# Gated linear attention on one core: new engine orders, and every second turned probability tile copied by ScalarE

## Chip, cores and metric

The kernel runs on one core of one Trainium2 chip. The metric is the device time of one launch in microseconds (us), lower is better. Engines are called PE (TensorE), ACT (ScalarE), DVE (VectorE), POOL (GpSimd) and SP (SyncE) below, as the profile calls them.

## The reference, cut to what matters

The program is two layers of a hybrid decoder over 1024 tokens of width 1024. The change lies in the token mixer of the first layer, chunked gated linear attention (GLA) with 4 heads (key width 96, value width 192), which runs in parallel with a 4-head cross-attention into 256 memory tokens:

```python
b = jnp.cumsum(log_a, axis=2)                     # per chunk of 64 tokens
att = einsum('bnihk,bnjhk->bnhij', q * exp(b - b_ref), k * exp(b_ref - b))
o_intra = einsum('bnhij,bnjhv->bnihv', where(tril, att, 0), v)
def step(state, xs):                              # over the chunks
    o = einsum('bchk,bhkv->bchv', qc, state)
    state = dc[..., None] * state + einsum('bchk,bchv->bhkv', kc, vc)
o = rms_norm(o_intra + o_inter, o_norm) * silu(og)
# memory cross-attention, 4 heads of 64, beside it:
p = softmax(einsum('bshd,bmhd->bhsm', q, k) * 64 ** -0.5)
o = einsum('bhsm,bmhd->bshd', p, v)
```

## The kernel before, in words

`gla_phase` (a function of about 430 lines) is one stage of the program, some 180 us of its 2520. Every engine has its own hand-written list of work; they meet only at semaphores. The stage takes the heads h = 0 to 3 in turn.

**PE.** For each head: `gate` (gate projection of the next head, L2508), `token_products` (L2517 within a pair of chunks, L2522 across it), the rest of `project` (L2499, query and key projections of the next heads, in 8 slices d; only for heads 1 and 2, since head 3 is gathered from columns computed with the others), `state_changes` (eight turns of the keys, L2532, then seven products, L2539), `project` again, and `outputs` (fifteen matmuls, L2551 and L2554).

**DVE.** For each head: `cross_pair` (L2417 to L2420), `sums_of` (the log gate L2371, a running sum L2372, two subtractions L2377 and L2378), `low` (the low part of a weight piece, L2366), `states` (L2427, L2429), four `product` calls (L2391, L2393, L2406), `outputs` (L2438, the scaled result).

**ACT.** `gate_in` (L2276, L2277), copies of the scores `att` out of PSUM (L2323), `gate_out` (Exp L2282, Ln L2285), `copy` and `high` (L2266, L2257), copies of the turned keys (L2333), `factor` (Exp, L2294), and the squares of the outputs (L2350). POOL masks `att` (L2237) and computes `rstd` in two halves of each head (L2244, L2246). Exp and Ln each need another table, so ACT loads one where it passes from one to the other.

**Cross-attention** (`CrossUnits`) is cut into 16 units (a unit is 128 tokens and 2 heads) and into 19 steps. In step s PE computes the scores of unit s (L1996), turns the probabilities of unit s-2 with four transposes into one PSUM bank, `t_bank` (L2004), and multiplies unit s-3 with the values (L2013). DVE takes the maximum of unit s (L2021), copies the turned probabilities of unit s-2 out of PSUM (L2029), takes a reciprocal (L2030) and scales unit s-3 (L2036). ACT computes the Exp of unit s (L2048). Since there is one `t_bank`, a turn waits for the copy of the turn before it. The steps are dealt out to places between the GLA work by the table `CROSS`; before, no step stands earlier than after the outputs of head 1:

```python
CROSS = {(1, "out"): range(0, 3), (2, "att"): range(3, 5), (2, "state"): range(5, 8), (2, "out"): range(8, 11),
         (3, "att"): range(11, 13), (3, "state"): range(13, 16), (3, "out"): range(16, CrossUnits.STEPS)}
```

**The ring.** Everything but the projections and the scores of the cross-attention goes through four PSUM banks, taken in turn: entry i waits for whoever frees entry i-4 (`ring_wait`). The two output banks of the first half of a head's outputs and the two of the second half are such entries, freed by DVE's `outputs`.

After the stage comes the output projection (`out_phase`); its first PE work, turns of input rows (L1317), starts when all engines have left the stage.

Of the kernel before, what the change touches and what calls it, by code (L numbers as in the profile page):

```python
# [30 lines left out]
DC = D // P  # L31
# [1938 lines left out]
class CrossUnits:  # L1970
# [8 lines left out]
    def __init__(self, nc, ctx, ph, psum, ident, q_of, keys, vals, out_of, room, sums, banks, out_bank):  # L1979
        def sem(name):  # L1980
            return phase_semaphore(nc, ctx, f"{ph}_{name}")

        self.nc, self.psum, self.ident, self.q_of, self.keys, self.vals, self.out_of = nc, psum, ident, q_of, keys, vals, out_of
        self.probs, self.probs_t, self.banks, self.out_bank = room[0:3], room[3:5], banks, out_bank
        self.neg_top, self.total = sums[:, 0:2 * self.PAIRS], sums[:, 2 * self.PAIRS:4 * self.PAIRS]
        self.scored, self.topped, self.expd = sem("scored"), sem("topped"), sem("expd")
        self.turned, self.turn_out, self.mixed = sem("turned"), sem("turn_out"), sem("mixed")
        self.inverted, self.out_done = sem("inverted"), sem("out_done")

    def pe(self, pe, s, ring_wait):  # L1990
        nc, (s_banks, t_bank) = self.nc, self.banks
        if s < self.PAIRS:
            t, i = divmod(s, 2)
            if s >= 2:
                pe.wait_ge(self.expd, s - 1)
            nc.tensor.matmul(self.psum[:, s_banks[s % 2], :], self.q_of(t, i), self.keys[:, 2 * i:2 * i + 2, :].rearrange("p h n -> p (h n)"),  # L1996
                             start=True, stop=True).then_inc(self.scored, 1)
        u = s - self.T_LAG
        if 0 <= u < self.PAIRS:
            pe.wait_ge(self.expd, u + 1)  # L2000
            if u >= 1:
                pe.wait_ge(self.turn_out, u)
            for c in range(4):
                turn = nc.tensor.transpose(self.psum[:, t_bank, c * P:(c + 1) * P], self.probs[u % 3][:, c, :], self.ident[:, :])  # L2004
            turn.then_inc(self.turned, 1)
        u = s - self.O_LAG
        if 0 <= u < self.PAIRS:
            pe.wait_ge(self.turn_out, u + 1)
            ring_wait(u)
            for e in range(2):  # L2010
                cols = slice((2 * (u % 2) + e) * XA_DIM, (2 * (u % 2) + e + 1) * XA_DIM)
                for c in range(2):
                    mm = nc.tensor.matmul(self.out_bank(u)[:, e * XA_DIM:(e + 1) * XA_DIM], self.probs_t[u % 2][:, 2 * e + c, :],  # L2013
                                          self.vals[:, c, cols], start=c == 0, stop=c == 1)
            mm.then_inc(self.mixed, 1)

    def dve(self, dve, s):
# [6 lines left out]
        if 0 <= u < self.PAIRS:  # L2024
            two = slice(2 * u, 2 * u + 2)
            dve.wait_ge(self.turned, u + 1)
            if u >= 2:
                dve.wait_ge(self.mixed, u - 1)
            nc.vector.tensor_copy(self.probs_t[u % 2], self.psum[:, t_bank, :].rearrange("p (c n) -> p c n", c=4)).then_inc(self.turn_out, 1)  # L2029
            nc.vector.reciprocal(self.total[:, two], self.total[:, two]).then_inc(self.inverted, 1)  # L2030
# [8 lines left out]
    def act(self, act, s):  # L2039
        if s >= self.PAIRS:  # L2040
            return
        act.wait_ge(self.topped, s + 1)
# [10 lines left out]
def gla_phase(nc, ph, psum, ident, neg_half, hT_hi, hT_lo, w_in, w_gate2, b_gate, rank_rows, V, Y, room, first_parts, last_rows, cross_room, pieces,  # L2053
# [10 lines left out]
    with ExitStack() as ctx:  # L2064
# [3 lines left out]
        def sem(name):  # L2068
# [53 lines left out]

        CROSS = {(1, "out"): range(0, 3), (2, "att"): range(3, 5), (2, "state"): range(5, 8), (2, "out"): range(8, 11),
                 (3, "att"): range(11, 13), (3, "state"): range(13, 16), (3, "out"): range(16, CrossUnits.STEPS)}

# [30 lines left out]
        for h in range(GLA_HEADS):  # L2156
            if h + 1 < GLA_HEADS:
                enter("z", "act", 2, h + 1)
            enter("att", "act", 2, h)
            enter("cross", "dve", 1, h)  # L2160
            enter_cross(h, "att")
            enter("keys", "act", 2, h)
            enter("delta", "state", 4, h)
            enter_cross(h, "state")
            enter("out", "dve", 4, h)
            enter_cross(h, "out")
# [16 lines left out]

        def at(h, kind, i=0):
            return entry_of[h, kind] + i

# [64 lines left out]
        def _(act):  # L2251
# [62 lines left out]
            for h in range(GLA_HEADS):  # L2314
# [21 lines left out]
                if more:  # L2336
                    factor(h + 1, 0)
                    factor(h + 1, 1)
                cross_steps(cross.act, act, h, "state")
                if fresh:  # L2340
                    copy(h + 1, 1)
                if h + 2 < LAST:
                    high(2 * h + 4)
                if h:
# [10 lines left out]
        def _(dve):  # L2355
# [11 lines left out]

            def sums_of(h):

                dve.wait_ge(softened, h + 1)  # L2370
                chain(nc.vector.scalar_tensor_tensor(soft, z, 0.0, soft, ALU.min, ALU.subtract))  # L2371
                chain(nc.vector.tensor_tensor_scan(cum, keep, soft, 0.0, ALU.mult, ALU.add))  # L2372
                c = cum.rearrange("p (c i) -> p c i", i=CHUNK)
# [58 lines left out]

            def outputs(h):
                for p in range(PAIRS):
                    if p % (PAIRS // 2) == 0:
                        dve.wait_ge(rstd_ready, 2 * h + 1 + p // (PAIRS // 2))
                    y = Y[:, p, h * DV:(h + 1) * DV]
# [4 lines left out]

            dve.wait_ge(kept, 2)
            sums_of(0)
            low(2)
# [3 lines left out]
            product(0, 3)  # L2449
            for h in range(GLA_HEADS):  # L2450
                more = h + 1 < GLA_HEADS
                fresh = h + 1 < LAST
                cross_pair(h)
                cross_steps(cross.dve, dve, h, "att")
                if more:
                    sums_of(h + 1)
                if fresh:
                    low(2 * h + 3)
                states(h)
                cross_steps(cross.dve, dve, h, "state")  # L2460
                if more:
                    product(h + 1, 0)
                if h + 2 < LAST:
                    low(2 * h + 4)
                if more:
                    product(h + 1, 1)
                outputs(h)
                if more:
                    product(h + 1, 2)
                    product(h + 1, 3)  # L2470
                if h == 1:
                    for part in range(2):
                        dve.wait_ge(parked[part], 16 * LAST)
                cross_steps(cross.dve, dve, h, "out")

        @block.tensor
        def _(pe):
# [47 lines left out]

            def state_changes(h):
                pe.wait_ge(factored, h + 1)
                for i in range(2):
                    ring_wait(at(h, "keys", i))
                    for c in range(4):  # L2530
                        p = 4 * i + c
                        mm = nc.tensor.transpose(bank(at(h, "keys", i))[:, c * DK:(c + 1) * DK], k_out[:, p * P:(p + 1) * P], ident[0:DK, 0:DK])  # L2532
                    mm.then_inc(mixed, 1)
                for p in range(PAIRS - 1):
                    i = at(h, "delta", p // 2)
# [7 lines left out]

            def outputs(h):
                pe.wait_ge(masked, h + 1)
                for p in range(PAIRS):
                    i = at(h, "out", p // 2)
# [21 lines left out]
            for h in range(GLA_HEADS):  # L2569
                if h + 1 < GLA_HEADS:  # L2570
                    gate(h + 1)
                token_products(h)
                if h + 1 < LAST:
                    project(2 * h + 2, range(EARLY, DC))
                cross_at(h, "att")
                state_changes(h)
                cross_at(h, "state")
                if h + 1 < LAST:
                    project(2 * h + 3)
                outputs(h)  # L2580
# [723 lines left out]
```

## Time and profile before

| | us |
|---|---|
| median of 3 runs | 2525.84 |
| lowest, highest of the runs | 2524.62, 2526.70 |
| profiled execution, its time | 2521.81 |
| profiled execution, its span | 2520.00 |
| head loop of the stage starts (PE) | 248.15 |
| first cross-attention scores (PE) | 316.43 |
| last DVE instruction of the stage ends | 405.47 |

The span is the time from the first to the last instruction on the core; the execution's own time is 1.81 us longer. The rows further down are from the trace of that one execution. "Idle before" is the time in which an engine stood still ahead of an instruction, with the instruction that released it. The granted clock is 1.00 where PE had its full clock (2.4 GHz) and 0.50 where it had the lower level (1.2 GHz).

### The profile page before, as it was taken

How to read it: one execution, taken by the hardware profiler on the slowest of the kernel's cores; microseconds unless marked ns; L12 is line 12 of the kernel's file. 1: busy time of each engine (PE TensorE's matmuls, PEld its weight loads, DVE VectorE, ACT ScalarE, POOL GpSimd, SP SyncE). 2: the span in 40 equal slices, each digit the busy share in tenths (PEclk: the TensorE clock that was granted, in tenths of full speed). 3: DMA queues.
4: the chain of work that ended last, by engine and by line, in shares of the span. 5: the costliest groups of instructions: out<-in, count | busy, mean ns of one | idle time of the engine just before them, and what ended most of it. 6: DMA issues, size and time to landing. Idle time of an engine off the chain costs nothing. (4 is left out here: it accounts for less than half of the span.)

```text
span 2520.0 us, 32372 instructions
## 1 busy us (share of the span) xinstructions
PE 2432.4 (97%) x11700; PEld 2055.1 (82%) x11700; DVE 1729.7 (69%) x2908; ACT 1033.7 (41%) x2126; POOL 225.7 (9%) x271
## 2 busy tenths in 40 slices
PE   7999979999999999998999999999899999999998
PEld 7998757888888887777889889887788888888777
DVE  4532564379899888885553562463669999898896
ACT  6433443344444443335434432333334444443443
POOL 1010021000000000041212021122100000000000
PEclk9999988999999999999999999999999999999999
DMA  4330121322222248743102011212532222226764
GB/s 149 89 89 22 39 79 43 100 69 84 76 92 84 75 142 272 262 142 130 51 17 81 35 34 42 60 34 73 168 115 75 85 84 83 77 91 221 280 200 146
DMA packets 207541, 257.72 MB, mean 102 GB/s; under 512 B 38376, under 2 KB 141784, under 8 KB 207384
## 3 DMA queue, kind: packets, MB, share of 16 engines
q1 hardware_dynamic: 203224, 255.65, 31.0%
q8 instruction: 94, 1.54, 0.3%
q10 hardware_dynamic: 4160, 0.02, 0.1%
q14 instruction: 63, 0.52, 0.1%
HBM read 206.54 MB, written 49.09 MB: 101 GB/s over the span
## 5 line engine op out<-in xcount | busy, mean ns | idle before, releaser
L52 PE MATMUL psum<-f_T_lo 128*128 128x512 f32 x616 | 244.6, 397 | 13.0 <-DVE f_T_lo L676 11.9
L53 PE MATMUL psum<-f_T_lo 128*128 128x512 f32 x616 | 241.3, 392 | 0.0
L54 PE MATMUL psum<-f_T_lo 128*128 128x512 f32 x616 | 241.2, 392 | 0.0
L52 PE MATMUL psum<-w_hi,hT_hi 128*128 128x512 f32 x576 | 229.3, 398 | 4.2 <-DVE w_lo L1445 2.5
L54 PE MATMUL psum<-w_hi,hT_lo 128*128 128x512 f32 x576 | 226.3, 393 | 0.0
L53 PE MATMUL psum<-w_lo,hT_hi 128*128 128x512 f32 x576 | 226.1, 393 | 0.0
L52 PEld LDWEIGHTS psum<-f_T_lo 128*128 128x128 f32 x616 | 116.4, 189 | 48.1 <-DVE f_T_lo L676 21.1
L52 PEld LDWEIGHTS psum<-w_hi,hT_hi 128*128 128x128 f32 x576 | 124.8, 217 | 22.4 <-issue 3.9
L54 PEld LDWEIGHTS psum<-w_hi,hT_lo 128*128 128x128 f32 x576 | 125.0, 217 | 17.9
L53 PEld LDWEIGHTS psum<-w_lo,hT_hi 128*128 128x128 f32 x576 | 125.1, 217 | 16.6
L52 PE MATMUL psum<-hT_hi,f_up_hi 128*128 128x512 f32 x352 | 137.4, 390 | 0.4 <-DVE f_up_lo L615 0.4
L54 PE MATMUL psum<-hT_hi,f_up_lo 128*128 128x512 f32 x352 | 137.0, 389 | 0.0
L53 PE MATMUL psum<-hT_lo,f_up_hi 128*128 128x512 f32 x352 | 137.0, 389 | 0.0
L54 PEld LDWEIGHTS psum<-f_T_lo 128*128 128x128 f32 x616 | 116.4, 189 | 25.0
L53 PEld LDWEIGHTS psum<-f_T_lo 128*128 128x128 f32 x616 | 116.4, 189 | 23.1
L52 PE MATMUL psum<-T_hi,f_s_hi 128*128 128x512 f32 x320 | 124.5, 389 | 0.0
L53 PE MATMUL psum<-f_T_lo,f_s_hi 128*128 128x512 f32 x320 | 124.5, 389 | 0.0
L54 PE MATMUL psum<-T_hi,f_s_lo 128*128 128x512 f32 x320 | 124.5, 389 | 0.0
L52 PE MATMUL psum<-T_hi,f_up_hi 128*128 128x512 f32 x320 | 124.5, 389 | 0.0
L53 PE MATMUL psum<-f_T_lo,f_up_hi 128*128 128x512 f32 x320 | 124.5, 389 | 0.0
L54 PE MATMUL psum<-T_hi,f_up_lo 128*128 128x512 f32 x320 | 124.5, 389 | 0.0
L455 ACT ACTIVATE f_T_lo<-f_up_pieces 128x1024 fp32r<-128x1024 f32 (+1 forms) x72 | 67.0, 957 | 119.1 <-PE psum L54 101.9
(416 smaller groups left out, 6087.7 us busy)
## 6 DMA issues: line engine op xcount, KB each, us to landing
raw<-in_ffn_w_up_dram SPq DMA_DIRECT2D x88, 512.0 KB, 4.7
activations<-f_act SPq DMA_DIRECT2D x44, 512.0 KB, 2.6
f_up_pieces<-activations SPq DMA_DIRECT2D x38, 512.0 KB, 4.4
w_raw<-in_b_w_in_dram SPq DMA_DIRECT2D x18, 1024.0 KB, 5.9
f_up_pieces<-in_ffn_w_down_dram SPq DMA_DIRECT2D x20, 512.0 KB, 4.8
x_between<-XY SPq DMA_DIRECT2D x16, 512.0 KB, 5.2
XY<-x_between SPq DMA_DIRECT2D x16, 512.0 KB, 6.5
f_up_pieces<-activations SPq DMA_DIRECT2D x28, 256.0 KB, 3.9
```

What stands on the lines that cost most here:

```text
L52: nc.tensor.matmul(out, lhs_hi, rhs_hi, start=start, stop=False)
L53: nc.tensor.matmul(out, lhs_hi, rhs_lo, start=False, stop=False)
L54: return nc.tensor.matmul(out, lhs_lo, rhs_hi, start=False, stop=stop)
L455: nc.scalar.activation(hi, raw, ACT.Copy).then_inc(b_high, 1)
```

## The change

- `CrossUnits`: the copy of the turned probabilities stays on DVE for even units and goes to ACT (an activation with Copy) for odd units. The semaphore `turn_out` becomes two, one for even and one for odd units. On ACT the copy of unit s-2 stands behind the Exp of unit s.
- The steps move: 0 and 1 go between the two halves of the outputs of head 1 (new place "half"), step 2 stays behind them; steps 5 and 13 go to a new place "keys", between the turns of the keys and the state products; step 16 goes between the halves of the outputs of head 3.
- PE: `state_changes` is split; the keys are turned (`turn_keys`) before the last slice of the first projection of a head, and `outputs` comes in halves.
- ACT: the key copies come before `copy` and `high`; for head 3, `factor` moves between the squares of the two halves of head 2's outputs; the cross steps of "att" come before the key copies.
- DVE: `sums_of` is split (`logs_of`), the outputs come in halves with products 2 and 3 between them for heads 0 and 1, and for heads 2 and 3 the order is written out.

```diff
+    def wait_turn_out(self, eng, u):
+        eng.wait_ge(self.turn_out[u % 2], u // 2 + 1)
...
             if u >= 1:
-                pe.wait_ge(self.turn_out, u)
+                self.wait_turn_out(pe, u - 1)
...
-            dve.wait_ge(self.turned, u + 1)
-            if u >= 2:
-                dve.wait_ge(self.mixed, u - 1)
-            nc.vector.tensor_copy(self.probs_t[u % 2], ...).then_inc(self.turn_out, 1)
+            if u % 2 == 0:
+                dve.wait_ge(self.turned, u + 1)
+                if u >= 2:
+                    dve.wait_ge(self.mixed, u - 1)
+                nc.vector.tensor_copy(self.probs_t[0], self.turned_tile()).then_inc(self.turn_out[0], 1)
+            else:
+                dve.wait_ge(self.expd, u + 1)
...
     def act(self, act, s):
+        u = s - self.T_LAG
+        if s < self.PAIRS:
+            self.act_exp(act, s)
+        if 0 <= u < self.PAIRS and u % 2:
+            act.wait_ge(self.turned, u + 1)
+            if u >= 2:
+                act.wait_ge(self.mixed, u - 1)
+            self.nc.scalar.activation(self.probs_t[1], self.turned_tile(), ACT.Copy).then_inc(self.turn_out[1], 1)
...
+        CROSS = {(1, "half"): range(0, 2), (1, "out"): range(2, 3), (2, "att"): range(3, 5), (2, "keys"): range(5, 6), (2, "state"): range(6, 8),
+                 (2, "out"): range(8, 11), (3, "att"): range(11, 13), (3, "keys"): range(13, 14), (3, "state"): range(14, 16),
+                 (3, "half"): range(16, 17), (3, "out"): range(17, CrossUnits.STEPS)}
...
-                if fresh:
-                    copy(h + 1, 0)
-                    high(2 * h + 3)
+                cross_steps(cross.act, act, h, "att")
...
-                cross_steps(cross.act, act, h, "att")
-                if more:
+                if fresh:
+                    high(2 * h + 3)
+                    copy(h + 1, 0)
+                cross_steps(cross.act, act, h, "keys")
+                if fresh:
                     factor(h + 1, 0)
                     factor(h + 1, 1)
...
+                    if p == PAIRS // 2:
+                        if more and not fresh:
+                            factor(h + 1, 0)
+                            factor(h + 1, 1)
+                        cross_steps(cross.act, act, h, "half")
...
+            for h in range(LAST - 1):
                 cross_pair(h)
+                logs_of(h + 1)
+                sums_of(h + 1)
+                low(2 * h + 3)
                 states(h)
+                product(h + 1, 0)
                 if h + 2 < LAST:
                     low(2 * h + 4)
+                product(h + 1, 1)
+                cross_steps(cross.dve, dve, h, "half")
+                outputs(h, 0)
+                product(h + 1, 2)
+                product(h + 1, 3)
+                outputs(h, 1)
...
+            cross_steps(cross.dve, dve, LAST - 2, "out")
+            first, second, third = CROSS[LAST - 1, "out"]
+            cross_pair(LAST - 1)
+            cross_steps(cross.dve, dve, LAST - 1, "att")
+            cross_steps(cross.dve, dve, LAST - 1, "keys")
+            logs_of(LAST)
+            states(LAST - 1)
+            cross.dve(dve, CROSS[LAST - 1, "state"][0])
+            sums_of(LAST)
+            cross.dve(dve, CROSS[LAST - 1, "state"][1])
+            outputs(LAST - 1, 0)
+            product(LAST, 0)
+            cross.dve(dve, first)
+            product(LAST, 1)
+            outputs(LAST - 1, 1)
+            cross.dve(dve, second)
+            product(LAST, 2)
+            product(LAST, 3)
+            cross.dve(dve, third)
+            cross_pair(LAST)
...
...
-                if h + 1 < LAST:
-                    project(2 * h + 2, range(EARLY, DC))
+                if fresh:
+                    project(2 * h + 2, range(EARLY, DC - 1))
                 cross_at(h, "att")
+                turn_keys(h)
+                if fresh:
+                    project(2 * h + 2, range(DC - 1, DC))
+                cross_at(h, "keys")
                 state_changes(h)
                 cross_at(h, "state")
...
-                outputs(h)
+                outputs(h, 0)
                 if h == 1:
                     pe.wait_ge(copied, 2 * LAST)
                     pe.wait_ge(kv_loaded, 16 * len(kv_loads))
+                cross_at(h, "half")
+                outputs(h, 1)
                 cross_at(h, "out")
```

## Rows read from the trace of the kernel before

**Rows 1.** The page, busy time of each engine over the whole span.
```profile
PE 2432.4 (97%) x11700; PEld 2055.1 (82%) x11700; DVE 1729.7 (69%) x2908; ACT 1033.7 (41%) x2126; POOL 225.7 (9%) x271
```

**Rows 2.** Windows: us, busy us (instructions) of each engine, granted clock.
```profile
316.40:330.70 14.30, 8.39 (x16) 2.93 (x14) 7.54 (x16) 4.95 (x18) 8.17 (x6) 0.68 0.84 321
330.70:355.10 24.40, 21.57 (x125) 16.99 (x125) 16.81 (x32) 14.56 (x32) 1.10 (x1) 0.84 0.00 1
```

**Rows 3.** Timeline of PE: start, duration, work, idle before in brackets.
```profile
261.38 2.49 PE L2539 MATMUL psum<-gla_v,gla_k_rows 128*96 128x192 f32 x14 [1.87 <-ACT gla_k_rows L2333]
...
316.43 1.88 PE L1996 MATMUL psum<-kv_room,xqT 128*128 128x512 f32 x4
324.22 2.08 PE L1996 MATMUL psum<-kv_room,xqT 128*128 128x512 f32 x2 [5.91 <-ACT cross_room L2048]
...
330.73 3.78 PE L2517 MATMUL psum<-gla_q_mid,gla_k_mid 96*128 96x128 f32 x16
...
367.48 1.08 PE L2004 MATMUL psum<-ident,cross_room 128*128 128x128 f32 x4 [4.21 <-DVE cross_room L2029]
...
373.55 2.00 PE L2517 MATMUL psum<-gla_q_mid,gla_k_mid 96*128 96x128 f32 x16
...
400.75 1.08 PE L2004 MATMUL psum<-ident,cross_room 128*128 128x128 f32 x4 [2.79 <-DVE cross_room L2029]
...
405.80 1.94 PE L1317 MATMUL psum<-ident,XY 128*128 128x128 f32 x8 [0.65 <-PEq L2064]
```

**Rows 4.** Timeline of PE, one undisturbed cross-attention step at full clock.
```profile
385.61 0.60 PE L2004 MATMUL psum<-ident,cross_room 128*128 128x128 f32 x4
386.05 1.00 PE L2013 MATMUL psum<-kv_room,cross_room 128*128 128x64 f32 x8
386.89 1.08 PE L1996 MATMUL psum<-kv_room,xqT 128*128 128x512 f32 x2
```

**Rows 5.** Windows of 2 us; the clock is the third last figure.
```profile
338.00:340.00 2.00, 2.00 (x14) 1.75 (x13) 1.80 (x5) 0.46 (x1) 1.10 (x1) 0.83 0.00 0
...
346.00:348.00 2.00, 1.32 (x6) 0.56 (x5) 1.93 (x5) 1.39 (x5) 0.00 (x0) 1.00 0.00 0
...
372.00:374.00 2.00, 2.00 (x16) 2.00 (x16) 1.71 (x4) 1.02 (x4) 0.00 (x0) 0.80 0.00 0
```

**Rows 6.** Timeline of DVE.
```profile
261.00 1.21 DVE L2366 TENSOR_TENSOR mem_lo<-kv_room,mem_lo 128x1024 fp32r<-128x1024 f32 x1
...
322.43 1.28 DVE L2021 TENSOR_REDUCE rank_rows<-psum 128x2 f32<-128x512 f32 x2
...
405.18 0.29 DVE L2036 TENSOR_TENSOR XY<-psum,rank_rows 128x128 f32<-128x128 f32 x1 [1.41 <-PE psum L2013]
```

**Rows 7.** Timeline of POOL.
```profile
317.73 1.01 POOL L2246 TENSOR_TENSOR gla_rstd<-gla_sums,neg_half 128x4 f32<-128x4 f32 x1
```

**Rows 8.** Groups of ACT, 316.4 to 405.8 us: busy, mean ns | idle.
```profile
L2048 ACT ACTIVATE cross_room<-psum,rank_rows 128x256 f32<-128x256 f32 x32 | 14.8, 473 | 25.0 <-DVE rank_rows L2021 25.0
L2323 ACT ACTIVATE gla_att<-psum 128x512 f32<-128x512 f32 x4 | 2.4, 597 | 3.1 <-PE psum L2517 3.1
L2276 ACT ACTIVATE raw<-psum,gla_bias 96x512 f32<-96x512 f32 x2 | 1.4, 683 | 1.5 <-PE psum L2508 1.5
L2285 ACT ACT_TABLE_LOAD x1 | 1.3, 1283 | 0.0
L2285 ACT ACTIVATE gla_soft<-gla_soft 96x1024 f32<-96x1024 f32 x1 | 1.1, 1057 | 0.0
```

**Rows 9.** Groups of DVE, 316.4 to 405.8 us.
```profile
L2429 DVE SCALAR_TENSOR_TENSOR gla_state<-gla_state,gla_decay,psum 96x192 f32<-96x192 f32 x12 | 4.9, 410 | 0.4
L2029 DVE COPY cross_room<-psum 128x512 f32<-128x512 f32 x8 | 5.5, 686 | 0.3 <-PE psum L2004 0.3
L2406 DVE TENSOR_TENSOR gla_k_out<-gla_k_mid,gla_ends 96x1024 f32<-96x1024 f32 x2 | 2.4, 1216 | 0.0
L2372 DVE TENSOR_TENSOR_SCAN raw<-gla_keep,gla_soft 96x1024 f32<-96x1024 f32 x1 | 2.3, 2286 | 0.0
```

More of the change, by code:

```diff
@@ L1986, in __init__, with turned_tile @@
         self.scored, self.topped, self.expd = sem("scored"), sem("topped"), sem("expd")
-        self.turned, self.turn_out, self.mixed = sem("turned"), sem("turn_out"), sem("mixed")
+        self.turned, self.mixed = sem("turned"), sem("mixed")
+        self.turn_out = [sem(f"turn_out_{n}") for n in ("even", "odd")]
         self.inverted, self.out_done = sem("inverted"), sem("out_done")
+    def wait_turn_out(self, eng, u):
+        eng.wait_ge(self.turn_out[u % 2], u // 2 + 1)
+    def turned_tile(self):
+        return self.psum[:, self.banks[1], :].rearrange("p (c n) -> p c n", c=4)
     def pe(self, pe, s, ring_wait):
@@ L2162, in gla_phase @@
             enter("keys", "act", 2, h)
+            enter_cross(h, "keys")
             enter("delta", "state", 4, h)
             enter_cross(h, "state")
-            enter("out", "dve", 4, h)
+            enter("out", "dve", 2, h)
+            enter_cross(h, "half")
+            enter("out_end", "dve", 2, h)
             enter_cross(h, "out")
@@ L2184, in at @@
         def at(h, kind, i=0):
+            if kind == "out" and i >= 2:
+                return entry_of[h, "out_end"] + i - 2
             return entry_of[h, kind] + i
@@ L2343, in _ @@
                     high(2 * h + 4)
+                cross_steps(cross.act, act, h, "state")
                 if h:
@@ L2431, in states, with outputs @@
                     dve.wait_ge(state_ready, (PAIRS - 1) * h + p + 1)
-            def outputs(h):
-                for p in range(PAIRS):
+            def outputs(h, half):
+                for p in range(half * PAIRS // 2, (half + 1) * PAIRS // 2):
                     if p % (PAIRS // 2) == 0:
-                        dve.wait_ge(rstd_ready, 2 * h + 1 + p // (PAIRS // 2))
+                        dve.wait_ge(rstd_ready, 2 * h + 1 + half)
                     y = Y[:, p, h * DV:(h + 1) * DV]
@@ L2443, in _ @@
             dve.wait_ge(kept, 2)
+            logs_of(0)
             sums_of(0)
@@ L2463, in _ @@
                 if h + 2 < LAST:
                     low(2 * h + 4)
-                if more:
-                    product(h + 1, 1)
-                outputs(h)
[L2468 to L2474, printed above, removed]
+                product(h + 1, 1)
+                cross_steps(cross.dve, dve, h, "half")
@@ new lines, in _ @@
+                outputs(h, 0)
+                product(h + 1, 2)
+                product(h + 1, 3)
+                outputs(h, 1)
+            for part in range(2):
+                dve.wait_ge(parked[part], 16 * LAST)
+            cross_steps(cross.dve, dve, LAST - 2, "out")
[4 more added lines that the diff above has]
+            logs_of(LAST)
@@ new lines, in _ @@
+            states(LAST - 1)
[12 more added lines that the diff above has]
+            cross_pair(LAST)
+            cross_steps(cross.dve, dve, LAST, "att")
@@ L2476, in _ @@
+            cross_steps(cross.dve, dve, LAST, "keys")
+            states(LAST)
+            cross_steps(cross.dve, dve, LAST, "state")
+            cross_steps(cross.dve, dve, LAST, "half")
+            outputs(LAST, 0)
+            cross.dve(dve, CROSS[LAST, "out"][0])
+            outputs(LAST, 1)
+            cross.dve(dve, CROSS[LAST, "out"][1])
         @block.tensor
@@ L2542, in state_changes, with outputs @@
                         mm.then_inc(mixed, 1)
-            def outputs(h):
+            def outputs(h, half):
                 pe.wait_ge(masked, h + 1)
-                for p in range(PAIRS):
+                for p in range(half * PAIRS // 2, (half + 1) * PAIRS // 2):
                     i = at(h, "out", p // 2)
```

31 lines of the change are left out of this document (8 added, 23 removed).

## The prediction, made before the changed kernel was run

> **What bounds the kernel now.** I read the page first: PE is busy 97% of the span [rows 1], so a gain has to be PE time won, and since the later stages keep PE full, time won in this stage passes through to the end. Next the windows of the stage. Up to 316.4 us PE is nearly full; from 316.4 to 330.7 it is busy 8.4 of 14.3 us at a mean clock of 0.68, and the next 24.4 us have 0.84 [rows 2]. PE's timeline shows why [rows 3]: a wait of 1.87 us for the key copies at 261.38 (the same again in head 1), one of 5.91 us at 324.22 for ACT's first Exp, of 4.21 us at 367.48 and of 2.79 us at 400.75 for DVE's copy. The first big one is DVE's fault: PE has issued scores 0 and 1 by 318.3, but DVE takes the first maximum at 322.43 [rows 6], after the outputs and two products of head 1. Third, the clock: after the waits of 5.91 and 4.21 us the work runs at half clock (score pairs 2.08 instead of 1.08 us, rows 3 and 4 compared) [rows 3, 4], and the full clock is back only at 338.7 and 372.8 (from the means 0.83 and 0.80 of their windows) [rows 5]. A wait thus costs itself and half of the slow stretch behind it.
>
> **The change, part by part.** I walk the queues from head to head with durations from the rows, 0.05 us a handoff.
>
> *Keys turned early (heads 0 and 1).* The last slice of the projection (six matmuls, 1.36 us) now covers ACT's two key copies, so the 1.87 us [rows 3] go. What is late next is `project` 3, which waits for `low`: that ends at 262.2, because its DVE predecessors are unchanged [rows 6]. The state products now end at 261.55, so PE stands 0.7 us: gain 1.3 us (263.57 to 262.26). Head 1 starts 1.3 earlier, its keys give 1.3 again: 2.6 us. Bounds: 0 if `low` slips by as much, 3.7 if it never waits.
>
> *Steps 0 and 1 between the output halves of head 1.* The first half of the outputs ends on PE at 311.2. The memory keys must have landed by then: before, PE showed no wait for them at 316.43 [rows 3], so a late landing can cost at most the 5.2 us between. Scores 0 and 1 run 311.2 to 313.2, DVE's maxima 312.4 to 313.9, the Exps to 314.9, while PE does the second half (to 315.75). DVE then has outputs, products 2 and 3 (2 x 1.14 us apart) [rows 9], and waits for the second `rstd`: squares end 316.6, POOL takes 1.01 [rows 7] and two short steps, so outputs end at 319.4. PE goes from step 2 (with a turn) through the gate projection to `token_products` of head 2 at 319.0, against 330.73 [rows 3]: 11.7 us gained so far, the 2.6 included, because the wait of 5.91 and its half clock are gone. If the `rstd` wait moved the whole of it back, 5 would remain.
>
> *The odd copy on ACT: a new wait.* One copy of 128x512 costs DVE 0.69 us; ACT's copies of that shape took 0.60 [rows 8, 9]. The copy itself is cheap; its place isn't. Maximum 2 comes at 320.1 (behind the outputs), Exp 2 to 321.05. ACT then has `gate_in` (four of 0.68, 2.3 with overlap), two score copies (1.1), `gate_out` (Exp, a table of 1.28, Ln 1.06: 3.4), a table load of 1.28, Exp 3 (two halves 0.47 and their reads: 0.9) [rows 8], and only then the copy of unit 1, done at 330.65. The turn of unit 2 needs it, since there is one `t_bank`; behind that turn stand, in PE's queue, unit 1's product, the key turns and everything of head 2. PE has nothing from 325.3 on: a new wait of 5.4 us. DVE waits too, for the turn, with unit 2's copy. Before, this copy was DVE's and `gate_out` overlapped with step 3. Bounds: 2 us if ACT's work is spread better than I think, 7 if handoffs are slow.
>
> *What the new wait does to the clock.* 5.4 us lies between the 4.21 and 5.91 that both lost the clock. The slow busy stretch was 5.3 us behind the one and 14.5 behind the other [rows 3, 5]; what follows here (turn, product, scores) is like the shorter case. From 330.7 at half clock for 5.3 us costs 2.7; I take 8 us of it, 4. Ends: 0 (the clock stays) and 7.
>
> *Head 2's rest.* `logs_of` before `states`, `sums_of` (2.29 scan, a short and a long subtraction, 3.6) [rows 9] after step 6. With 2.7 of clock loss: states 339.4 to 342.4 (seven of 0.4 in sequence [rows 9]), maximum 6, copy 4, running sums to 347.5, maximum 7, Exp 7 at 349.05, ACT copy 5, squares of the first half to 350.85, `factor` 2.5 to 353.35, squares to 354.55, second `rstd` at 355.9. PE meanwhile has outputs to 349.9, then waits of 1.7 (unit 5's product for a ring bank that DVE's outputs free), 1.3 (for copy 6), and 2.7 (for copy 7, which is behind Exp 9, behind maximum 9, behind DVE's outputs). `token_products` of head 3 start at 362.3, against 373.55: 11.2 ahead.
>
> *Head 3 and the tail.* Steps 11 to 18 are PE-bound at about 2.2 us (0.43 + 0.84 + 0.93, starts in [rows 4]), but for 1.2 at step 12 waiting for ACT's copy 9. Step 16's place hides what waited 2.79 us and then ran at half clock at 400.75 [rows 3]. DVE ends at 391.1, against 405.47 [rows 6]: 14.4 ahead. The row turns that follow (1.94 us at half clock [rows 3]) may find full clock: 0.9. The added semaphore, the reciprocals and POOL's mask (1.1 us, 15 us of slack) I cost at nothing; POOL's weight splits cover more of the stage but end before they are needed.
>
> *The sum.* 14.4 + 0.9 = 15.3; minus 1.3 for the longer slow stretch, minus 1 for handoffs I count low over some 20 links: **13.0 us**. Against the profiled execution's own 2521.81 that is 2508.8. The median of the runs lies 4.0 above that execution, so the same gain gives 2525.84 - 13.0 = **2512.8**.
>
> *A rule against it.* Gaps of 1.56 us and less in a stretch that was 66% busy left the clock at 1.00 (1.32 of 2 us) [rows 5]; the new order has 1.7, 1.3 and 2.7 close together between 350 and 361. The Trainium skill, TensorE: Matmul & The Clock Gate, section "A second HAM failure mode: psum-queue depth-cycling", says that frequent micro-idles between matmul groups that cycle through PSUM banks make the clock oscillate. By that rule the cross steps from 331 on would run mostly slow; rival 3 prices it, and the row so far speaks against it.
>
> **Rivals.**
> 1. *The clock is lost a second time*, at the 2.7 us wait for copy 7 near 361. For it: 2.79 us at 400.75 was followed by half clock (4 turns 1.08) [rows 3]. Against: the wait at 346 to 348 wasn't. At half clock for 5 to 8 us: 2.5 to 4 more, gain 7 to 11, about 2516.5.
> 2. *No clock loss at the first wait*, or a shorter wait since ACT overlaps more: 13.0 + 4 gives 17, 2508.8. Against: both waits over 4 us lost it.
> 3. *The clock stays low, and the kernel gets slower.* Place: all PE work after 330.7, which by my list is 47 us at full clock with 9 us of waits in it. Slow work swallows the waits. It decides from the point where over 62% of the 47 us run at half clock: 330.7 + 47 x 1.62 + 3 = 410, past 405.5 + 5. With all of it slow, 330.7 + 94 + 3 = 428, 22 us late: 2548. Against it: 342 to 355 had waits every few us and kept 1.00 after 340.
> 4. *The change gives little* (it doesn't do what it says): each of the 8 odd copies waits out its Exp and itself (0.9 + 0.6, 1.5 us), 12 us, with none hidden, and steps 0 and 1 still stall on DVE. Then 1 to 5 us are left, about 2523. Against: in the walk only copies 1, 7 and 9 are seen by PE.
>
> **How the numbers follow.** Likeliest case (gain 11 to 16) 0.50; rival 1 0.26; rival 2 (16 to 19) 0.12; rival 3 0.04; rival 4 0.08, half of it inside 0.2%. 0.2% is 5 us, which is about what a measurement of this kernel can tell from no change. The range from a gain of 7 to one of 19 holds the first three: 2507 to 2519. Faster by over 0.2%: 0.50 + 0.26 + 0.12 + 0.03 = 0.91; within: 0.05; slower: 0.04.
>
> **What the profile after would show.** Right: `token_products` of head 2 near 319, and ahead of it no wait over 1 us; key-copy waits under 1 us; one PE wait of about 5.4 us before a turn (L2004's code) near 325 to 331, released by the Copy on ACT; half clock behind it; full clock from about 339; three waits under 3 us between 350 and 361; head 3's `token_products` near 362; the next stage's turns near 391. Wrong: a wait at the memory keys' semaphore; the turn of unit 2 released before 328; half clock through the 350s; a later stage longer than before, which none of my terms has.

## The result and the profile after

The changed kernel takes 2507.31 us (median of 7 runs, 2504.89 to 2512.37) against 2524.62 (7 runs, 2516.76 to 2526.70). The ratio is 0.9942, 95% interval 0.9931 to 0.9953: 14.6 us faster, between 11.9 and 17.4. In the profiled executions the span went from 2520.0 to 2505.8 us, 14.2 less. The next stage's first PE work starts at 391.74 instead of 405.80 [rows 3], 14.1 earlier, so in these two profiles the gain was won before that point. Below this number is called the *stage mark*.

On the page after, PE is busy 2428.7 us, 97% of the span again, against 2432.4 [rows 1]:

```profile
PE 2428.7 (97%) x11700; PEld 2053.4 (82%) x11700; DVE 1725.7 (69%) x2900; ACT 1036.6 (41%) x2134; POOL 226.0 (9%) x271
```

The work is the same. Eight copies changed sides (DVE 2908 to 2900 instructions, ACT 2126 to 2134). Here is PE's timeline after, with its waits in the stage but for two of 0.20 and 0.33 us. The number in brackets is the idle time ahead. L2573 is the old L2517, L2012 are the turns, L2021 the products with the values, L2555 the projections:

```profile
264.88 0.73 PE L2555 MATMUL psum<-h_hi,mem_lo 128*128 128x512 f32 x2 [0.19 <-DVE mem_lo L2397]
300.44 0.73 PE L2555 MATMUL psum<-h_hi,mem_lo 128*128 128x512 f32 x2 [0.41 <-DVE mem_lo L2397]
322.06 3.15 PE L2573 MATMUL psum<-gla_q_mid,gla_k_mid 96*128 96x128 f32 x16 [0.65 <-DVE XY L2470]
333.75 0.63 PE L2012 MATMUL psum<-ident,cross_room 128*128 128x128 f32 x4 [2.04 <-ACT gla_v L2058]
344.04 0.63 PE L2012 MATMUL psum<-ident,cross_room 128*128 128x128 f32 x4 [0.64 <-DVE cross_room L2038]
353.39 1.08 PE L2021 MATMUL psum<-kv_room,gla_v 128*128 128x64 f32 x8 [1.63 <-DVE XY L2470]
356.37 0.63 PE L2012 MATMUL psum<-ident,cross_room 128*128 128x128 f32 x4 [0.98 <-DVE cross_room L2038]
361.19 0.63 PE L2012 MATMUL psum<-ident,cross_room 128*128 128x128 f32 x4 [2.45 <-ACT gla_v L2058]
369.78 0.63 PE L2012 MATMUL psum<-ident,cross_room 128*128 128x128 f32 x4 [0.96 <-ACT gla_v L2058]
391.74 1.94 PE L1317 MATMUL psum<-ident,XY 128*128 128x128 f32 x8 [1.68 <-PEq L2083]
```

The waits of 1.87 (twice), 5.91, 4.21 and 2.79 us [rows 3] are gone. In their place stand three behind ACT's new copies (2.04, 2.45, 0.96, released by L2058) and two over 0.7 us behind DVE (1.63 and 0.98). Windows of 2 us show where the clock was lost before the tail of the stage (the clock is the third figure from the end):

```profile
250.00:252.00 2.00, 2.00 (x15) 2.00 (x15) 0.00 (x0) 2.00 (x4) 0.00 (x0) 0.76 0.00 0
252.00:254.00 2.00, 2.00 (x18) 1.78 (x17) 0.00 (x0) 1.51 (x3) 0.00 (x0) 0.50 0.00 0
...
322.00:324.00 2.00, 1.94 (x12) 1.97 (x13) 1.83 (x5) 0.80 (x3) 1.10 (x2) 0.68 1.03 418
324.00:326.00 2.00, 1.80 (x12) 1.50 (x11) 0.00 (x0) 2.00 (x6) 2.00 (x1) 0.50 1.02 420
...
332.00:334.00 2.00, 0.25 (x2) 0.28 (x3) 0.89 (x4) 1.99 (x9) 0.67 (x1) 1.00 0.00 0
```

It was lost where PE had no gap (at 251, 2.00 of 2.00 us busy) or a short one (0.65 us ahead of 322.06), and not at the wait before 333.75, where PE was busy 0.25 of 2 us; from 334 to 390 us it stayed at 1.00. That is not how I had it. A second profile of the same kernel (after_again, below) shows what I had forecast: the clock lost behind the wait.

### The profile page after: what moved, and what is told of

It is laid out like the page before. It is cut to its first block and busy times, and to the rows that moved or that the text cites. A ratio compares the mean times of both kernels' runs of the same rounds, so it can differ in the third digit from the quotient of the medians.

```text
span 2505.8 us, 32380 instructions
## 1 busy us (share of the span) xinstructions
PE 2428.7 (97%) x11700; PEld 2053.4 (82%) x11700; DVE 1725.7 (69%) x2900; ACT 1036.6 (41%) x2134; POOL 226.0 (9%) x271
```

## The experiments

Times are given as the ratio to the kernel before, measured beside it on the same chip. The median of before was between 2520.5 and 2524.6 us, so 0.001 is 2.5 us. The stage mark comes from one profile each and contains that execution's luck with the clock. Names that end in "_again" are the same kernel measured a second time.

| kernel | ratio (95% interval) | stage mark | head 2's, head 3's token products |
|---|---|---|---|
| before | 1 | 405.80 | 330.73, 373.55 |
| changed | 0.9942 (0.9931 to 0.9953) | 391.74 | 322.06, 362.50 |
| after_again | 0.9958 (0.9944 to 0.9973) | 395.82 | 319.34, 363.28 |
| keys_early_only | 0.9984 (0.9973 to 0.9995) | 407.74 | 330.98, 375.49 |
| half_only | 0.9984 (0.9973 to 0.9995) | 400.78 | 323.77, 368.54 |
| only_act_copy | 1.0028 (1.0014 to 1.0043) | 408.48 | 330.46, 375.68 |
| all_copies_dve | 0.9922 (0.9904 to 0.9941) | 385.02 | 319.31, 356.73 |
| all_copies_dve_again | 0.9924 (0.9911 to 0.9938) | 388.36 | 319.34, 357.10 |
| copy_first | 0.9913 (0.9899 to 0.9928) | 384.45 | 319.44, 355.92 |
| copy_first_again | 0.9909 (0.9896 to 0.9923) | 383.28 | 319.42, 354.75 |
| gate_late | 0.9919 (0.9905 to 0.9933) | 387.10 | 322.18, 358.56 |
| step3_first | 0.9960 (0.9948 to 0.9972) | 393.56 | 319.21, 358.99 |
| splits_later | 0.9941 (0.9926 to 0.9956) | 396.18 | 319.69, 363.61 |
| waits_filled | 0.9941 (0.9928 to 0.9953) | 388.96 | 319.41, 359.73 |

**One part alone: the keys.** The lists of PE and ACT in short:

```diff
 PE: -  project(2 * h + 2, range(EARLY, DC)); cross_at(h, "att"); state_changes(h)
     +  project(2 * h + 2, range(EARLY, DC - 1)); cross_at(h, "att"); turn_keys(h)
     +  project(2 * h + 2, range(DC - 1, DC)); state_changes(h)
 ACT: -  copy(h + 1, 0); high(2 * h + 3); key copies
      +  key copies; high(2 * h + 3); copy(h + 1, 0)
```

> The kernel before with the keys turned ahead of the last projection slice (PE), and ACT's key copies ahead of its copy of the projection. Theory 1: both waits of 1.87 us go and 0.2 to 0.7 us for the low part comes instead, 1.3 us for each head, 2.6 us faster in all, since PE is full up to 316. Rival (the project call that follows is late by as much): 0. A difference of 2.6 us is 0.1% and near what the runs can tell, so the trace decides: the start of head 1's second projection and the start of the first scores, 316.4 before.

Measured: 0.16% faster, 1.3 to 6.8 us. In its profile the key waits are gone, but the clock fell near 251 us with PE full, so that single trace shows no earlier second projection of head 1 (300.78 us). In after_again, where it didn't fall there, that projection starts at 297.70, against 300.48 in the kernel before (its timeline): 2.8 us. Up to there the changed kernel differs in the place of the keys and in the orders of ACT and DVE around them, so the term of 2.6 stands.

**One part alone: steps 0 and 1.**

```diff
-CROSS = {(1, "out"): range(0, 3), ...
+CROSS = {(1, "half"): range(0, 2), (1, "out"): range(2, 3), ...
 DVE, head 1:
-  outputs(h); product(h + 1, 2); product(h + 1, 3)
+  steps of "half"; outputs(h, first half); product(h + 1, 2); product(h + 1, 3); outputs(h, second half)
```

> The kernel before with cross steps 0 and 1 between the output halves of head 1, on all three engines, DVE's outputs of that head in halves around products 2 and 3. Theory 1: the wait of 5.9 us and most of the half clock behind it go; head 2's token products start 8 to 9 us earlier, near 322; 7 to 10 us faster at the end. Rival (the stall is only moved: DVE's outputs are late, PE waits for ring banks): token products of head 2 after 327 and less than 4 us faster.

Measured: 0.16% faster, 4.0 us (1.3 to 6.8), less than the 7 to 10 expected. The token products of head 2 do start 7.0 us earlier, nearly as theory 1 says, in spite of a stretch at half clock near 263. Of these, 2.0 are given back by the stage mark (5.0 earlier). PE's timeline:

```profile
323.77 2.02 PE L2526 MATMUL psum<-gla_q_mid,gla_k_mid 96*128 96x128 f32 x16 [0.65 <-DVE XY L2440]
327.13 1.15 PE L2531 MATMUL psum<-gla_q_in,gla_k_out 96*64 96x64 f32 x16 [1.33 <-ACT gla_soft L2277]
334.35 1.09 PE L2004 MATMUL psum<-ident,cross_room 128*128 128x128 f32 x4 [2.83 <-DVE gla_v L2029]
...
362.45 1.09 PE L2004 MATMUL psum<-ident,cross_room 128*128 128x128 f32 x4 [4.21 <-DVE cross_room L2029]
```

A head start puts PE ahead of the engines that feed it: two new waits (1.33 for the gate's reads on ACT, 2.83 for DVE's copy 1), and a turn of 1.09 us, half clock, behind the second. The later waits of 4.21 and 2.79 stay as they were. They are gone in the changed kernel and, with every copy on DVE, in all_copies_dve too, so it is the orders of heads 2 and 3 that take them away.

No run has these orders alone. By subtraction they are the largest part: with all copies on DVE the new orders bring 19 to 20 us (ratios 0.9922 and 0.9924, below), and the two parts above brought 4.0 each by themselves, which leaves 11 to 12 us. That is an estimate from these ratios, and it holds only if the parts add up.

**One part alone, and one part undone: the copies on ACT.** only_act_copy has the odd copies on ACT in the old orders (with ACT's cross steps of "att" ahead of the key copies; left where they were, the engines would wait for one another); all_copies_dve is the changed kernel with no copy on ACT:

```diff
+    def on_act(self, u):
+        return False
...
-            if u % 2 == 0:
+            if not self.on_act(u):
```

> The kernel before with odd copies on ACT, and for that ACT's cross steps of the place att moved ahead of its key copies (with the old place the engines would wait for one another). Nothing else moved. Theory 1: the wait of 5.9 us for Exp 0 and the half clock behind it stay; copies 1, 7 and 9 are late behind Exps, copy 0 stays on DVE: between 3 us slower and 2 us faster than before. Rival: 5 us or more faster.

> The changed kernel with every copy of turned probabilities back on DVE; all new orders kept. Theory 1 (the orders bring the gain, the ACT copy costs PE a wait and saves DVE 0.69 us eight times): the wait of 2.04 us for ACT's copy 1 goes, but Exp 3 still ends near 333 behind the gate work, so PE waits there one step later, 1 to 2 us; between 350 and 361 DVE is the late engine and gets copies 5 and 7 (1.3 us) more. Sum within 2 us of the changed kernel, 12 to 16 us under the kernel before. Rival (the ACT copy is what brings the gain): 5 us or more of the 14.6 are lost, 2514 or more where the kernel before has 2524.

Both speak against the copy on ACT. Alone it makes the kernel 0.28% slower (3.5 to 10.8 us; I had between 2 faster and 3 slower). Undone, the changed kernel gains: 0.9922, then 0.9924, against 0.9942 and 0.9958. These were measured on different chips, each beside the kernel before, and the lower interval of the changed kernel touches the other two; but every pairing points the same way, by some 4 to 9 us. My "within 2 us" was wrong. The rival, that this copy brings the gain, has fallen.

PE's wait before the turn of unit 2 doesn't go with ACT's copy. It is now for DVE's copy of unit 1, 2.19 us in the first profile (0.69 in the second, where PE was at half clock just before), and the turn starts earlier, at 329.24 instead of 331.03 in after_again. The wait for copy 7 is 1.51 instead of 2.45:

```profile
329.24 0.63 PE L2015 MATMUL psum<-ident,cross_room 128*128 128x128 f32 x4 [2.19 <-DVE gla_v L2041]
...
355.42 0.63 PE L2015 MATMUL psum<-ident,cross_room 128*128 128x128 f32 x4 [1.51 <-DVE gla_v L2041]
```

> All copies on DVE once more, beside copy_first. If the place of the copy in its queue is what counts and not the engine, the two are within 2 us of each other, and both 5 to 11 us faster than the changed kernel.

**The changed kernel again.**

> The changed kernel once more, for a second profile beside the others of this call. Theory 1 says that the stage starts its last turns (next stage's first PE work) at 391.7 us less whatever the clock does differently: the half clock at 251 to 257 us of the first profile is chance, so 389 to 392. If ACT's copies cost more than they save (all copies on DVE gave 0.9922), the ratio stays above 0.993.

The ratio of 0.9958 is 10.6 us (6.8 to 14.1) against 14.6 in the first measurement, and above 0.993 as expected. The stage mark of 395.82 lies outside the 389 to 392 that I gave: its trace shows that the first profile's mark was on the lucky side. PE's timeline, and then the clock in 2 us windows:

```profile
322.69 1.15 PE L2578 MATMUL psum<-gla_q_in,gla_k_out 96*64 96x64 f32 x16 [1.32 <-ACT gla_soft L2303]
331.03 0.63 PE L2012 MATMUL psum<-ident,cross_room 128*128 128x128 f32 x4 [3.95 <-ACT gla_v L2058]
...
361.63 0.63 PE L2012 MATMUL psum<-ident,cross_room 128*128 128x128 f32 x4 [2.45 <-ACT gla_v L2058]
...
395.82 1.14 PE L1317 MATMUL psum<-ident,XY 128*128 128x128 f32 x8 [1.67 <-PEq L2083]
```
```profile
330.00:332.00 2.00, 0.97 (x9) 1.00 (x9) 0.30 (x1) 1.80 (x7) 0.00 (x0) 0.96 0.00 0
332.00:334.00 2.00, 2.00 (x13) 2.00 (x13) 0.75 (x3) 0.27 (x1) 0.00 (x0) 0.50 0.00 0
...
338.00:340.00 2.00, 2.00 (x13) 1.96 (x13) 1.44 (x3) 0.31 (x1) 0.00 (x0) 0.84 0.00 0
...
362.00:364.00 2.00, 2.00 (x14) 2.00 (x13) 2.00 (x5) 0.81 (x3) 0.00 (x0) 0.64 0.00 0
...
372.00:374.00 2.00, 2.00 (x10) 1.47 (x10) 0.29 (x1) 1.19 (x5) 1.91 (x3) 0.80 0.00 0
```

With the clock up at 319, PE reaches the wait for copy 1 earlier and waits 3.95 us; half clock follows from about 331.8 to 338.6 (worked out from the window means). It comes again after the wait of 2.45, from about 362.6 to 372.8. Both waits stand behind ACT's copy. In this execution each cost itself and half of the seven or ten microseconds at half clock. splits_later, below, whose PE list is the same, has the same two waits and the same two slow stretches.

**Where the copy stands in ACT's queue.** In the changed kernel ACT's list around copy 1 is this (timeline, reads of the accumulator left out):

```profile
327.34 1.08 ACT L2308 ACTIVATE gla_soft<-gla_soft 96x1024 f32<-96x1024 f32 x1
328.44 1.28 ACT L2311 ACT_TABLE_LOAD   x1
329.73 1.06 ACT L2311 ACTIVATE gla_soft<-gla_soft 96x1024 f32<-96x1024 f32 x1
330.81 1.28 ACT L2067 ACT_TABLE_LOAD   x1
332.10 0.47 ACT L2067 ACTIVATE cross_room<-psum,rank_rows 128x256 f32<-128x256 f32 x1
...
333.01 0.59 ACT L2058 ACTIVATE gla_v<-psum 128x512 f32<-128x512 f32 x1
```

The copy loads no table of its own: here it follows an Exp directly, and in gate_late, below, one runs behind Ln (337.33 us) ahead of the next load (337.93). In this list it stands behind two loads of 1.28 us, and behind Exp 3. copy_first swaps the two of a step:

```diff
     def act(self, act, s):
         u = s - self.T_LAG
-        if s < self.PAIRS:
-            self.act_exp(act, s)
         if 0 <= u < self.PAIRS and u % 2:
             ... copy of unit u
+        if s < self.PAIRS:
+            self.act_exp(act, s)
```

> The changed kernel, but ACT takes the odd copy ahead of the Exp of the same step. Theory 1 (PE waits for copies 7 and 9 only because they stand behind Exps 9 and 11, which wait for DVE's maxima): the waits of 2.45 and 0.96 us go, copy 1 comes 1 us sooner, 2.5 to 4.5 us faster than the changed kernel. Rival (the Exps are then late instead, since each turn comes half a microsecond behind its scores): within 1 us of it.

> copy_first once more, for a second profile with the clock in another state. Theory 1: ratio 0.990 to 0.993; where the clock stays up before head 2's token products, PE waits 1 to 2 us for copy 1, and no copy after it makes PE wait over 1 us.

Measured: 0.9913 and 0.9909, some 7 to 12 us faster than the changed kernel (11 us in the one comparison on the same chip, 0.9913 against 0.9958), more than the 2.5 to 4.5 expected. The waits for copies 7 and 9 are gone in both profiles; the one for copy 1 is gone in the first and 1.61 in the second (PE's timeline):

```profile
328.78 0.63 PE L2012 MATMUL psum<-ident,cross_room 128*128 128x128 f32 x4 [1.61 <-ACT gla_v L2056]
339.41 0.63 PE L2012 MATMUL psum<-ident,cross_room 128*128 128x128 f32 x4 [0.64 <-DVE cross_room L2038]
348.28 1.08 PE L2021 MATMUL psum<-kv_room,gla_v 128*128 128x64 f32 x8 [1.15 <-DVE XY L2470]
```

The second profile has the full clock from 310 to 382 us, where after_again had two slow stretches; its mark is 12.5 us earlier. That is probably the difference to my number: I counted the waits, not the slow stretches behind them. The kernel with the copy first has the lowest ratios of the study, with medians of 2499.24 and 2500.15 us. Between it and all copies on DVE (0.9922, 0.9924) the runs don't decide: they are 2.3 and 3.8 us apart, not within the 2 that I expected, and the intervals overlap.

**The gate moved instead.** step3_first takes Exp 3 and copy 1 ahead of `gate_out` (and moves POOL's splits of weights as splits_later does, so it changes two things); gate_late is copy_first with steps 3, 4 and the key copies ahead of `gate_out` of head 3. ACT's lists in short:

```diff
 step3_first, ACT, head 2:  -gate_out(3); step 3; step 4; key copies
                            +step 3; gate_out(3); step 4; key copies
 gate_late, ACT, head 2:    -gate_out(3); step 3; step 4; key copies; step 5
                            +step 3; step 4; key copies; gate_out(3); step 5
```

> The changed kernel, but ACT takes step 3 (Exp 3, copy 1) ahead of gate_out of head 3, and POOL takes one weight split behind the mask of head 2 and three behind that of head 3 in place of two behind head 1's second rstd. Theory 1 (copy 1 is late because of gate_out and its two table loads): PE's wait before the turn of unit 2 (2.04 us) shrinks to under 1 us, and token products of head 3 start 1 to 3 us sooner after those of head 2. Rival (DVE's maximum 3 sets it): the wait stays over 1.5 us.

> Copy ahead of Exp as in copy_first, and for head 2 ACT does steps 3 and 4 and the key copies before gate_out of head 3. Theory 1: PE has no wait over 1 us between head 2's token products and its outputs, which start near 338 (345.3 in the changed kernel); DVE's logs wait for the late gate. 1 to 5 us faster than copy_first. Rival (the late gate delays sums, maximum 7, squares and factor, which set the later waits): token products of head 3 start no sooner than in copy_first, same time.

In step3_first the wait for copy 1 is 0.96 us, as theory 1 says, but the key copies now stand behind the gate and PE waits 1.73 us for them, and loses the clock there and again behind the wait of 2.45 that is left. From head 2's token products to head 3's it takes 39.8 us, against 40.4 and 43.9 in the two profiles of the changed kernel, but the kernel isn't faster (0.9960). gate_late removes the waits for copy 1 and for the keys, and has no gain over copy_first (0.9919). Head 2's outputs start at 344.52, not near 338. Ahead of them PE waits 1.33 for a ring bank that ACT's `gate_in` frees, 0.98 for a state and 1.56 for DVE's copy 4, with half clock behind the last; the two later ones fit logs that come late, which wasn't tested by itself. The outcome is the rival's: from head 2's token products to head 3's it is 36.4 us, and 36.5 and 35.3 in copy_first. That they start at 322.18 against 319.42 comes from a stretch at half clock from about 286.5 to 293 us.

**POOL against DVE.** POOL splits weights of a later stage (L1116, L1118) at the same place in both kernels. In the kernel before, DVE's first multiplication of `cross_pair` for head 2 came at 336.45, seven microseconds behind the last of them. With head 2 earlier, the two meet. The two timelines of the changed kernel, DVE first:

```profile
327.41 2.82 DVE L2449 TENSOR_TENSOR gla_q_in<-gla_q_in,gla_ends 96x512 f32<-96x512 f32 x1 [3.58 <-PE psum L2578]
```
```profile
327.34 2.34 POOL L1118 TENSOR_TENSOR h_lo<-o_w_stage,h_hi 128x1024 fp32r<-128x1024 f32 x1
```

splits_later moves the splits:

```diff
-SPLITS = {(1, "rstd"): range(0, 2), (3, "mask"): range(2, 4)}
+SPLITS = {(2, "mask"): range(0, 1), (3, "mask"): range(1, 4)}
```

> The changed kernel with only POOL's weight splits moved: one behind the mask of head 2, three behind that of head 3. In the changed kernel DVE's first multiplication of cross_pair of head 2 took 2.82 us in place of 0.69 while POOL ran a tensor_tensor of 2.34 us. If the two hold each other up, it is back at 0.69 here. Theory 1 (ACT is later still, so the 2.1 us are hidden): time within 1 us of the changed kernel. Rival (they are on the path): 2 us faster.

The same multiplication takes 0.69 us in this kernel (the row is below). The ratio, 0.9941, is that of the changed kernel within the intervals, and PE's wait for copy 1 is 3.95 us with the splits in the way (after_again) and without (this run): the delay was hidden behind ACT's later copy.

```profile
324.22 0.69 DVE L2449 TENSOR_TENSOR gla_q_in<-gla_q_in,gla_ends 96x512 f32<-96x512 f32 x1 [2.77 <-PE psum L2578]
```

**What a wait costs beyond itself.** waits_filled keeps PE at work in the waits for copies 1 and 7, with four and two more score products whose results nobody reads:

```diff
         pe.wait_ge(self.expd, u + 1)
+        for _ in range({4: 4, 10: 2}.get(s, 0)):
+            nc.tensor.matmul(self.psum[:, 2, :], self.q_of(0, 0), self.keys[:, 0:2, :]..., start=True, stop=True)
         if u >= 1:
             self.wait_turn_out(pe, u - 1)
```

> The changed kernel with spare work in two of PE's waits: four score products (0.93 us each) ahead of the wait for copy 1 and two ahead of the wait for copy 7, into a PSUM bank that nobody uses then and with results nobody reads. Nothing waits less. Theory 1 (a wait costs itself and the half clock behind it): the waits of 3.95 and 2.45 us shrink to under 0.6, the clock stays at 1.00 from 332 to 374 us, and the kernel is 3 to 8 us faster than the changed one though it does more work. Rival (the waits alone cost, and the clock falls by chance): same time, or slower by 1.

```profile
326.99 3.60 PE L2010 MATMUL psum<-kv_room,xqT 128*128 128x512 f32 x8
331.01 0.66 PE L2014 MATMUL psum<-ident,cross_room 128*128 128x128 f32 x4 [0.42 <-ACT gla_v L2060]
...
355.87 1.88 PE L2010 MATMUL psum<-kv_room,xqT 128*128 128x512 f32 x4
358.39 0.66 PE L2014 MATMUL psum<-ident,cross_room 128*128 128x128 f32 x4 [0.64 <-ACT gla_v L2060]
```

The turn of unit 2 starts at 331.01 as in after_again (331.03): the release is the same. But the clock stays at 1.00 from there to 388, head 3's token products start 3.6 us earlier than in after_again and the stage mark is 6.9 us earlier. Between these two traces, then, the two slow stretches are worth about 7 us. One trace of each doesn't show that filling the waits is what kept the clock: in the changed kernel's first profile neither wait lost it (the first was 2.04 us there). Nor do the runs: 0.9941 stands against 0.9942 and 0.9958, no difference that can be told, where I expected 3 to 8 us. Theory 1 isn't shown, and the rival isn't excluded.

A count over all fourteen profiles says more about which waits pay. It takes each wait of PE from the start of the stage to the stage mark (the one that ends at the mark left out), and asks whether the granted clock was at 0.50 two microseconds after PE's return:

| wait of PE | waits | half clock behind them |
|---|---|---|
| 3.95 to 5.91 us | 9 | 9 |
| 2.45 to 2.83 us | 10 | 8 |
| 1.51 to 2.19 us | 20 | 5 |
| 1.00 to 1.33 us | 13 | 0 |

So the price of a wait is paid in some executions and not in others, and in these profiles it was paid more often the longer the wait. The count shows what goes together, not the cause.

## Why the prediction was right, point by point

*The number.* 2512.8 was forecast with a range of 2507 to 2519, 13.0 us faster; measured 2507.31 and 14.6 by the ratio. The absolute time is 5.5 us lower than forecast, only 0.3 us inside the range: the median of the kernel before is itself 1.2 us lower in its 7 runs than in the first 3, and the two medians lie 17.3 us apart where the ratio gives 14.6. The second measurement of the same kernel gave 10.6, so the forecast of 13.0 lies between the two.

*Keys early, 2.6 us.* 2.8 in the profile that kept its clock there (after_again). The new wait for `low` is 0.42 and 0.41 in it; I had 0.7 for the first.

*Steps 0 and 1, token products of head 2 at 319.0.* 319.34 in after_again; 322.06 in the first profile, 2.7 later because of the half clock at 251 to 257 (second `project` of head 0 at 264.88 against 262.13). Alone, in the old orders, this part was worth 4.0 us where the expectation for half_only said 7 to 10. In the prediction's walk it was the first 9 of the 14 us; what the walk doesn't say is that without the later orders PE only runs into the next waits.

*The new wait for copy 1, 5.4 us.* Placed right, sized too long: 3.95 us where PE came to it at full clock. The walk missed that `token_products` waits 1.32 us for a ring bank that ACT's `gate_in` frees, so PE comes later to the wait (the row at 322.69 us above); the copy itself came within 0.4 us of the 330.65 forecast.

*Half clock behind it, 8 us.* 6.8 us in after_again, from 331.8 to 338.6. In the first profile it didn't follow; there the clock was lost at 251 and at 322, without a long wait ahead, and the stretch at 322 hid part of the wait instead (2.04 us). So in the profile whose sum came out right (mark 14.1 earlier, 14.4 and a little forecast) two slow stretches stood in for the forecast one: that agreement is in part luck. In after_again the forecast mechanism is there, but the mark is only 10.0 us earlier, because the clock was lost a second time, which is rival 1; the 10.6 us of its runs lie in that rival's 7 to 11.

*Head 2's later waits, 1.7, 1.3 and 2.7.* 1.63, 0.98 and 2.45, in their places. Copy 9 at step 12: 1.2 forecast, 0.96. Head 3's token products: 362.3 forecast, 362.50 and 363.28.

*Rival 1, the clock lost a second time at copy 7.* It happened in after_again (362.6 to 372.8), and behind the same wait of 2.45 in splits_later and step3_first, and not in the first profile. Its price of 2.5 to 4 us was too small: 10.2 us at half clock are 5.1. I gave it 0.26, as an alternative. It is better seen as something that each execution draws. The row that I set against it, the wait at 346 to 348 [rows 5], was no match: by the timeline that wait is 0.73 us.

*Rival 3 and the rule on micro-idles.* The Trainium skill, TensorE: Matmul & The Clock Gate, section "A second HAM failure mode: psum-queue depth-cycling", describes a clock that goes back and forth between its levels where PE idles briefly between groups. The first profile disagrees with that here: waits of 1.63, 0.98 and 2.45 us between 351 and 361 left the clock at 1.00. after_again went down behind the last of the three, and once only before the tail. No profile had most steps slow, which is what rival 3 priced. In its sum, 330.7 + 47 x 1.62 + 3 is 409.8, short of the 410.5 that it names; the bound would be 63%, not 62%.

*The tail.* End of the last DVE work forecast 391.1; measured 391.4 in the first profile, 395.5 in after_again. The turns of the next stage took 1.94 us again in the first profile and 1.14 in the second; my 0.9 us for them is also a matter of the draw.

*Costed at nothing: POOL's splits.* Nothing is what they cost, but not for the reason given. They held a DVE multiplication up by 2.1 us, and in after_again two of them by 2.75 in all; only the wait for copy 1 hid it.

*The sign of the ACT copy.* The prediction prices its wait but forecasts the whole change only. By the runs this part costs 4 to 9 us of what the orders bring, and its place behind the Exp is the reason, since the copy on ACT ahead of the Exp costs nothing that can be measured.

## What to carry to other kernels

Where an engine's queue is in order, an instruction that unblocks PE goes ahead of one that only has to be done soon; moving work to the idler engine (ACT was busy 41%) loses time if it lands behind a long list there, as in the changed kernel and in only_act_copy. Walk every queue past the moved instruction, ring banks included: in this case a walk with row durations placed four waits of head 2 and 3 within 0.35 us, and missed one for a ring bank that sized another 1.4 us too long. When one stall is removed, look at the next supplier in line, since a single early start of 7.0 us (half_only) was worth 4.0 in the runs.

## What the runs showed of the hardware that wasn't expected

- The granted clock fell to 0.50 at about 251 us in the changed kernel with PE busy 2.00 of 2.00 us in the windows 248 to 250 and 250 to 252, while it ran the gate projection (a 16-row operand, 16x512) and then the 96x128 token products; the same in keys_early_only, and in gate_late at about 286.5 us, at head 1's token products. At the same kind of work it fell near 319 to 323 in three profiles (changed, copy_first, all_copies_dve_again), with no wait over 0.7 us ahead. In after_again, the same kernel as changed, all these places kept 1.00. Why one execution loses it and another doesn't isn't settled by these runs.
- A DVE multiplication with both inputs in SBUF took 2.82 us instead of 0.69 when it started 0.07 us after a POOL subtraction of 2.34 us. The subtraction ended 2.27 us after the multiplication had begun, which leaves 0.55 us for the work. In after_again it was the next multiplication of the same shape, 2.83 us, started 0.39 us after a subtraction. DVE work that reads PSUM beside the same POOL instructions kept its time (in the kernel before a maximum of 0.69 us at 326.33 and a copy of 0.69 at 327.18, POOL busy from 325.78 to 329.24). The Trainium skill, SBUF — State Buffer, section "Summary: rules for kernel authors", says of a DVE operation with two SBUF inputs and a GpSimd one that reads SBUF that the second to issue fully blocks until the first finishes; the trace agrees with that.
- The part of the span behind the stage mark took from 2107.7 to 2117.2 us among the profiles, though the kernels are the same there (2114.2 before, 2114.1 after, 2110.0 in after_again). A part of a kernel should be compared by its own mark, in more than one profile, and a small difference by many runs.
